# High and low activations side by side: one 512-column product for two of the three passes

## What is computed

```python
def swiglu_ffn(h, w_in, w_out):              # hidden width 5632, twice
    g, u = jnp.split(h @ w_in, 2, axis=-1)
    return (jax.nn.silu(g) * u) @ w_out
...
q = rms_norm((h @ w_q).reshape(b, s, N_X_HEADS, X_HEAD_DIM), q_g)
```

## Time and profile before

| | us |
|---|---|
| median of 3 runs | 3943.48 (3941.76 to 3947.19) |
| the profiled execution | 3947.24 |
| its span, first to last instruction | 3945.5 |
| PE busy (share of the span) | 3680.2 (93%) |
| DVE busy | 2140.2 (54%) |
| ACT busy | 1617.5 (41%) |

### The profile page before, as it was taken

One profiled execution on the slowest core, in us unless ns is written; L12 is line 12 of the kernel. 1 busy time (PEld: TensorE's weight loads), 2 busy tenths in 40 slices (PEclk: granted clock), 3 DMA queues, 4 the chain that ended last, 5 costly groups with the idle time before them and its releaser, 6 DMA issues.

```text
span 3945.5 us, 60283 instructions
## 1 busy us (share of the span) xinstructions
PE 3680.2 (93%) x24695; PEld 3366.3 (85%) x24695; DVE 2140.2 (54%) x2737; ACT 1617.5 (41%) x2144; POOL 241.6 (6%) x232
## 2 busy tenths in 40 slices
PE   7888799999997999989999999999989899999998
PEld 6766799999977997768989989899777699899897
DVE  5887634555656545555444444554555554444444
ACT  4334323655643333444433333343333354333333
POOL 3562000000000020000000000000000000000000
PEclk9988899999998999989999999999998899999999
DMA  7324456555454564435656656555324356566564
GB/s 207 97 86 145 136 150 181 140 151 149 139 192 124 175 160 128 150 107 149 175 183 184 182 186 180 184 164 160 124 90 135 101 159 181 181 181 181 182 185 144
DMA packets 859333, 612.34 MB, mean 155 GB/s; under 512 B 10370, under 2 KB 752305, under 8 KB 858144
## 3 DMA queue, kind: packets, MB, share of 16 engines
q1 hardware_dynamic: 857072, 602.21, 52.3%
q0 software_dynamic: 2096, 7.81, 0.7%
HBM read 607.82 MB, written 2.16 MB: 155 GB/s over the span
## 4 chain that ended last, share of the span: by engine, by line
PE 83%; DVE 9%; ACT 3%; issue 2%; POOL 2%; DMA 0%; ACTq 0%; DVEq 0%; SPq 0%
PE acc L897 48%; PE acc L887 27%; PE psC L990 2%; DVE wL L1658 2%; PE psA L959 1%; ACT wH L1256 1%; DVE xtok L1619 1%; PE psC L945 1%; DVE arena L1965 1%; PE psB L945 1%; PE psB L973 1%; ACT L1256 1%; POOL arena L760 0%; PE psA L862 0%; DMA xtok<-in_x 0%
## 5 line engine op out<-in xcount | busy, mean ns | idle before, releaser
L1658 DVE TENSOR_TENSOR wL<-ring,wH 128x1024 fp32r<-128x1024 f32 x1128 | 1336.4, 1226 | 1125.3 <-ACT wH L1256 1120.6
L897 PE MATMUL acc<-actH,wH 128*128 128x256 f32 x5760 | 1654.8, 287 | 28.4 <-DVE wL L1658 28.4
L897 PE MATMUL acc<-actL,wH 128*128 128x256 f32 x5760 | 1632.4, 283 | 0.0
L897 PE MATMUL acc<-actH,wL 128*128 128x256 f32 x5760 | 1632.1, 283 | 0.0
L1256 ACT CAST wH<-ring 128x1024 fp32r<-128x1024 f32 x1128 | 1125.1, 1046 | 1223.2 <-PE acc L887 631.9
L897 PEld LDWEIGHTS acc<-actH,wH 128*128 128x128 f32 x5760 | 1108.3, 192 | 40.7 <-DVE wL L1658 23.0
L897 PEld LDWEIGHTS acc<-actL,wH 128*128 128x128 f32 x5760 | 1108.3, 192 | 4.8 <-issue 3.3
L897 PEld LDWEIGHTS acc<-actH,wL 128*128 128x128 f32 x5760 | 1107.7, 192 | 0.0
L887 PE MATMUL acc<-wH,actH 128*128 128x512 f32 x896 | 365.5, 408 | 25.9 <-DVE actL L1650 22.8
L887 PE MATMUL acc<-wL,actH 128*128 128x512 f32 x896 | 356.6, 398 | 0.0
L887 PE MATMUL acc<-wH,actL 128*128 128x512 f32 x896 | 355.7, 397 | 0.0
(11 more groups left out here) (294 smaller groups left out, 2488.1 us busy)
## 6 DMA issues: line engine op xcount, KB each, us to landing
ring<-in_w_ffn_in SPq DMA_DIRECT2D x176, 1024.0 KB, 5.7
ring<-in_w_ffn_out SPq DMA_DIRECT2D x88, 1024.0 KB, 5.1
ring<-in_b_w_in SPq DMA_DIRECT2D x64, 1024.0 KB, 6.2
ring<-in_w_in_ab SPq DMA_DIRECT2D x56, 1024.0 KB, 5.5
ring<-in_w_in_c SPq DMA_DIRECT2D x48, 1024.0 KB, 5.7
ring<-in_kv_w SPq DMA_DIRECT2D x24, 1024.0 KB, 5.6
ring<-in_a_w_in SPq DMA_DIRECT2D x16, 1024.0 KB, 7.1
ring<-in_w_xkv SPq DMA_DIRECT2D x16, 1024.0 KB, 5.7
```

Of the source, the lines that this page charges most:

```text
L897: ins = pe.matmul(dst, w[:, t, f * P:(f + 1) * P], x[:, t, :], start=t == 0 and n == 0, stop=t == ph.kt - 1 and n == 2)
L1658: dve.tensor_tensor(wL[:, split_slot, cols], ring[:, slot, cols], wH[:, split_slot, cols].bitcast(F32), ALU.subtract).then_inc(l_made, 1)
```

## The change

280 of the 360 "feat" blocks (all whose chunk is not drained through a silu or through ACT, and all of `ffn_in`) become "joined". High and low activations now lie side by side in one tile `act2`. For each of the 16 row tiles there are two matmuls in place of three: the high weight times 512 columns (high and low activations), whose halves land in the left and right half of a bank, and the low weight times the 256 high columns, added into the right half. Each block has a bank of its own. The chunk leaves PSUM in two steps: ACT copies the left halves of both banks to SBUF (`take_left`), DVE then adds the right halves (`add_right`). In the FFN the gate goes through ACT, DVE and then ACT again (silu, now from SBUF); the value chunk through ACT (copy), DVE (add), DVE (times silu, from SBUF).

```diff
+        self.joined, self.joined0 = joined, plan["joined"]
...
+        act2 = sb("act2", P, FT, 2, T, dt=F32R)
+        actH, actL = act2[:, :, 0, :], act2[:, :, 1, :]
...
+        def take_left(act, ph, i, c, dst):
+            act.wait_ge(blocks_done, ph.blocks_before(i, c, ph.blocks))
+            first = 2 * ph.pair(c)
+            act.copy(dst, acc[:, first:first + 2, 0:T]).then_inc(left_out, 1)
+        def add_right(dve, ph, i, c, dst, left):
+            dve.wait_ge(left_out, ph.lefts(i, c))
+            first = 2 * ph.pair(c)
+            return dve.tensor_tensor(dst, left, acc[:, first:first + 2, T:2 * T], ALU.add)
...
+                elif ph.joined:                                            # PE
+                    bank = pair[:, b, :]
+                    for t in range(ph.kt):
+                        pe.matmul(bank.rearrange("p (h t) -> p h t", h=2), high[:, t, :], act2[:, t, :, :],
+                                  start=t == 0, stop=False)
+                        ins = pe.matmul(bank[:, T:2 * T], low[:, t, :], xH[:, t, :], start=False,
+                                        stop=t == ph.kt - 1)
...
+                if b == ph.blocks - 1 and ph.joined:                       # ACT, after its casts
+                    take_left(act, ph, i, c, feat_slot(ph, fn, i, c))
...
                     def finish(i, c):                                      # ACT, FFN
                         if c == 0:
                             wait_past(act, drained[ffn_in.pair(1)], ffn_in.pair_uses(i, 1))
-                            act.activation(silu_g, src, ACT.Silu).then_inc(drained[ffn_in.pair(0)], 1)
+                            take_left(act, ffn_in, i, 0, silu_g)
                         else:
+                            act.wait_ge(drained[ffn_in.pair(0)], ffn_in.pair_uses(i, 0) + 1)
+                            act.activation(silu_g, silu_g, ACT.Silu).then_inc(silu_done, 1)
+                            take_left(act, ffn_in, i, 1, up_left)
                             act.wait_ge(drained[ffn_in.pair(1)], ffn_in.pair_uses(i, 1) + 1)
                             act.activation(hidH[:, bass.ts(i, 2), :], hid_f, ACT.Identity).then_inc(hid_h, 1)
...
-                        dve.wait_ge(drained[ffn_in.pair(0)], ffn_in.pair_uses(i, 0) + 1)
-                        dve.wait_ge(blocks_done, ffn_in.blocks_before(i, 1, 2))
-                        dve.tensor_tensor(hid_f, silu_g,
-                                          acc[:, 2 * ffn_in.pair(1), :].rearrange("p (f t) -> p f t", t=T),
-                                          ALU.mult).then_inc(drained[ffn_in.pair(1)], 1)
+                            if c == 0:
+                                add_right(dve, ffn_in, i, 0, silu_g, silu_g).then_inc(drained[ffn_in.pair(0)], 1)
+                        add_right(dve, ffn_in, i, 1, hid_f, up_left).then_inc(up_summed, 1)
+                        dve.wait_ge(silu_done, i + (pairs_done + 1))
+                        dve.wait_ge(up_summed, i + (pairs_done + 1))
+                        dve.tensor_tensor(hid_f, hid_f, silu_g, ALU.mult).then_inc(drained[ffn_in.pair(1)], 1)
```

More of the change, by code:

```diff
@@ L124, with __init__ @@
 class Dense:
-    def __init__(self, plan, src, kt, cols, blocks, chunks, style, iters=1, hidden=False):
+    def __init__(self, plan, src, kt, cols, blocks, chunks, style, iters=1, hidden=False, joined=False):
         self.src, self.kt, self.cols, self.blocks, self.style = src, kt, cols, blocks, style
@@ L132, in __init__ @@
         plan["chunks"] += chunks
+        self.joined, self.joined0 = joined, plan["joined"]
+        plan["joined"] += chunks if joined else 0
         self.end = plan["chunks"]
@@ L287, in program @@
         xoT = area(1024, XH, T)
-        silu_g, hid_f = ffn_tmp[:, 0, :, :], ffn_tmp[:, 1, :, :]
+        silu_g, hid_f, up_left = (ffn_tmp[:, k, :, :] for k in range(3))
         A_RE, A_IM, A_DT, A_D, A_BGLU = 0, 32, 64, 96, 104
@@ L347, in program @@
         out_done = sem("out_done")
-        plan = {"blocks": 0, "chunks": 0}
+        plan = {"blocks": 0, "chunks": 0, "joined": 0}
         def columns(w, kt, cols):
@@ L354, in columns, with feat @@
             return lambda j, k=0: v[:, k * kt:(k + 1) * kt, bass.ts(j, cols)]
-        def feat(w, first, tiles, iters=1):
+        def feat(w, first, tiles, iters=1, joined=True):
             at = columns(w, FT, P)
@@ L369, in tok @@
                          "tok", iters, hidden)
-        s5_u = feat(a["a_w_in"][0], 0, 8, 2)
-        s5_z = feat(a["a_w_in"][0], 8, 8, 2)
-        kv_mem = [(feat(a["w_xkv_2"][l], 0, XH), tok(a["w_xkv_2"][l], 1, 1, 4)) for l in range(DEPTH)]
+        s5_u = feat(a["a_w_in"][0], 0, 8, 2, joined=False)
+        s5_z = feat(a["a_w_in"][0], 8, 8, 2, joined=False)
+        kv_mem = [(feat(a["w_xkv_2"][l], 0, XH, joined=False), tok(a["w_xkv_2"][l], 1, 1, 4)) for l in range(DEPTH)]
         glu_at = columns(a["a_w_glu"][0], 8, 2 * P)
@@ L383, in program @@
             b_q.append(feat(a["b_w_in"][0], 8 * hh, 8, 2))
-            b_z.append([feat(a["b_w_in"][0], NH * (r + 1) + 8 * hh, 8, 2) for r in range(BRANCHES)])
+            b_z.append([feat(a["b_w_in"][0], NH * (r + 1) + 8 * hh, 8, 2, joined=False) for r in range(BRANCHES)])
         nsa_counts = [1] * 16 + [2] * 8 + [1] * 24
@@ L1266, in one_block @@
                                   i * (16 * ph.body * ph.blocks // SLOTS) + 16 * (n // SLOTS + 1), n)
-                if b == ph.blocks - 1 and fn is not None:
+                if b == ph.blocks - 1 and ph.joined:
+                    take_left(act, ph, i, c, feat_slot(ph, fn, i, c))
+                elif b == ph.blocks - 1 and fn is not None:
                     drain_chunk(act, ph, i, c, fn)
@@ L1447, in _ @@
             turn_out(TURN_LN1)
-            alternate(head_roots(norm_mem), join(*(block_steps(ph) for ph in kv_cmp)), [2, 2, 2, 2])
+            alternate(head_roots(norm_mem), join(*(block_steps(ph, dst) for ph, dst in zip(kv_cmp, (kcT, vcT)))),
+                      [2, 2, 2, 2])
             act.copy(mark[:, :], consts[:, 0:1]).then_inc(h_made, 2 * len(W1_BLOCKS))
@@ L1462, in _ @@
                            ACT.Sigmoid).then_inc(gate_ready, 1)
-            for ph in kv[1:]:
-                dense(ph)
-            dense(b_q[0])
+            dense(kv[1])
+            dense(kv[2], kwT)
+            dense(kv[3])
+            dense(b_q[0], qT)
             def silu_z(k):
@@ L1480, in _ @@
             alternate(attend(nsa_units), join(*(
-                [block_steps(b_z[0][r], silu_z(r)) for r in range(BRANCHES)] + [block_steps(b_q[1])] +
+                [block_steps(b_z[0][r], silu_z(r)) for r in range(BRANCHES)] + [block_steps(b_q[1], qT)] +
                 [block_steps(b_z[1][r], silu_z(BRANCHES + r)) for r in range(BRANCHES)])), nsa_counts)
@@ L1545, in tail_act @@
                                               i * 16 + 16 * (n // SLOTS + 1), n)
[L1546 to L1547 removed]
+                            finish(i, c)
                     pairs_done += ffn_in.iters
@@ L1553, in _ @@
             turn_out(TURN_MIX[1], G_MIX + 16)
-            dense(c_q)
-            blocks = join(block_steps(c_k), block_steps(c_v))
+            dense(c_q, dqT)
+            blocks = join(block_steps(c_k, dkT), block_steps(c_v))
             alternate(head_roots(norm_c), blocks, [2] * 8 + [1] * 4)
@@ L1665, in one_block @@
                     split_weights(n % SLOTS, n % SPLIT_SLOTS, ph.blocks_before(i, c, b) + 1)
-                if b == ph.blocks - 1 and fn is not None:
+                if b == ph.blocks - 1 and ph.joined:
+                    dst = feat_slot(ph, fn, i, c)
+                    add_right(dve, ph, i, c, dst, dst).then_inc(drained[ph.pair(c)], 1)
+                elif b == ph.blocks - 1 and fn is not None:
                     drain_chunk(dve, ph, i, c, fn)
```

33 lines of the change are left out of this document (20 added, 13 removed).

## The result

| | before | changed |
|---|---|---|
| median of 4 runs, us | 3942.62 | 4022.42 |
| lowest to highest | 3940.23 to 3947.19 | 4008.05 to 4026.12 |
| ratio, 95% interval | | 1.0194 (1.0167 to 1.0221) |
| span of the profiled execution | 3945.5 | 4022.5 |
| its mean granted clock | 0.967 | 0.954 |

A forecast was written before the change was run, and what follows sets the result against it. PE's matmul stream was taken as the bound. FFN +23.0, outside the FFN -6.9, clock +4.2 and +6.5 sum to +26.8 us, giving 3970 us on the median; range 3942 to 3996.

The forecast's parts named there:

- The matmuls: Joined blocks: 0.3474 us a pair, so 5.558 us a block in place of 5.760; 280 blocks save 56.6 us.
- The chain at the end of an iteration: FFN-in iteration ends, drain 1.47 us longer: +26.4 us over 24 boundaries (parts 2, 3), +23.4 over 14 (part 1).
- E: In an FFN-in iteration, the end of the value chunk's last matmul, from which the prediction counted PE's restart.
- The change to FFN-out: Ahead of each FFN-out PE waits for the low part, which comes 1.47 us later, 6 times: +8.8 us.
- Outside the FFN: Among head norms PE waits 0.64 us longer, 22 times: +14.1 us, against -21.0 from matmuls there: net -6.9.
- The clock: Longer PE stops lower the granted clock: +4.2 us at FFN-outs, +6.5 (bounds 0 and 20) at part 1's 14 stops.
- 16.1: Whole kernel with the clock left where it is, a rival: +16.1 us, 3959.6; chance 0.24.
- That rival: Every longer stop of PE lowers the clock: +39.9 us, 3983 us; chance 0.14.

The follow-up runs named there:

- x9: Changed kernel, its banks and drains kept, with the wide product split again into two of 256 columns; ratio 1.0294 to the kernel before.
- x4: Kernel before with only the 104 blocks outside FFN-in joined, FFN-in as before; ratio 1.0059 to the kernel before.
- x10: Changed kernel plus 8 unread 128-column matmuls in each head-norm step where PE waits for the drained chunk; ratio 1.0220 to the kernel before.
- x1: Changed kernel plus unread 512-column matmuls where PE waits in the FFN's first part and ahead of every FFN-out; ratio 1.0126 to the kernel before.
- x2: Changed kernel with the eight blocks of `kv_cmp` left unjoined, as before; ratio 1.0146 to the kernel before.
- x7: Kernel before plus one silu of one column on ACT ahead of the FFN's first loop; ratio 1.0005 to the kernel before.
- x12: Kernel before with FFN-in and 48 other blocks joined, early silu, second block's weight split earlier, products grouped in twos, unread matmuls ahead of FFN-out: ratio 0.9886, 3900.6 us.
- x5: Changed kernel with the products of two row tiles grouped as wide, wide, narrow, narrow; ratio 1.0152 to the kernel before.

## Why the prediction was wrong

The sign and the price of the drains were right, the size was not: 26.8 us forecast, 77 to 80 measured, outside the range. Two terms failed, the price of a pair and above all the clock. By the prediction's own steps:

- **The matmuls.** -56.6 forecast, from 0.3474 us a pair. That price exists (0.3467), but 177 of 280 blocks ran at 0.3533, at 0.107 a block saved in place of 0.202. Measured about -38. An error of 19 us, and one that I could not read before: no row had the mixture, and my bounds (5.12 to 5.76 us a block) held the value, 5.65. From the Trainium skill, TensorE: Matmul & The Clock Gate, section Back-to-back issue gap, I had estimated a saving of 0.04 us a block, which puts a block near 5.72 (5.76 less 0.04). Both measured blocks, 5.55 and 5.65, lie under it. The section gives its gap for an isolated matmul, which the prediction did not say.
- **The chain at the end of an iteration.** Right, but for the wait of 0.92 in place of 1.10 in parts 2 and 3. Part 2: PE restarts at E + 6.36 (forecast 6.40). Part 1: ACT's copy stands at 1873.58 in the chain, so E is 1873.49, and PE restarts at 1881.27, E + 7.78 (forecast 7.83):

```profile
1873.58 0.60 ACT ffn_tmp L546
...
1876.51 1.25 ACT L1289
...
1881.27 0.50 PE acc L918
```

- **The change to FFN-out.** Right: E is 2307.69 by the copy in the chain, PE starts at E + 4.22, where I had said some 4.2.

```profile
2307.78 0.59 ACT ffn_tmp L546
...
2310.88 0.70 DVE hidL L2179
2311.91 1.10 PE acc L911 x2
```

- **Outside the FFN.** The 0.64 per drain is there; at `kv_cmp`'s end, for instance, copy, sum and diagonals follow one another. x9 bears out the drains as a whole. The net of -6.9 became +23 (x4): fewer microseconds from the pairs, and the clock.

```profile
503.09 0.59 ACT arena L546
503.71 0.69 DVE arena L552
504.52 0.69 DVE probT L1739
```

- **The clock: the step that failed.** I took 4.2 + 6.5 = 10.7, with 19.6 as the upper bound of the part that I let vary. Measured +42 by the distances, +48.6 by halves. At FFN-out I had the count right (all six), but they cost 7.7 us more (492.8 together against 485.2), not 4.2, for some lost up to 2.8. I had the fourteen ends of part 1 as one in three at 1.4 us; seven of fourteen fell, at some 1.7 us (16 pairs of 0.460 in place of 0.353), 12 us. That is 20 in the FFN. What I left out, at nothing and without a reason, was everything else. I had priced waits among head norms by their length alone, 0.64 each, and not asked what they do to the clock: at `cmp_w1` and in the first `b_q` they cost some 14 us (the stretch is +16.5, and x10 with the same drains has +2.8; `cmp_w1` alone 10.5), and some 9 around `c_k` and `c_v` (+14.0, where x4 with the same instructions has +4.6). I also took 1.4 us as the price of any fall, from FFN-outs where PE streams at once; at `cmp_w1` the clock stayed at 0.50 for the whole of 27 us, though PE ran matmul after matmul. Why it does is open.

The sum with the measured sizes is 16.1 + 19 + 42 = 77 (84 with the clock by halves), against 77 in the profiles. That they meet to the microsecond is luck: at the 38 ends of iterations the slower block runs while PE would wait for `wL` anyway, which takes some 4 us off, and the clock's term is good to a few. That longer or added waits lower the clock is shown by x1, x2, x9 and x10; why the same instructions keep it in one run and lose it in another (x4, x7) is open.

Of what the Trainium skill describes in TensorE: Matmul & The Clock Gate, section HAM oscillation — how this bites in real kernels, a clock that falls at every wait between bursts, I had said that the trace agrees in part. It still does so in part: the clock fell at six of six changes to FFN-out, at seven of fourteen ends in part 1, where that rule has fourteen and I had between four and five, and in none of the second and third parts, although PE waits some 0.9 us in each of their iterations. That rival's 3983 us was nearer than my 3970, but neither held the waits outside the FFN.

## What to carry to other kernels

A wait of PE has two prices, its length and what the clock loses after it; the second was the larger here, some 42 us of 77. Read the granted clock at every place where a change lengthens a wait, not only at the longest ones, and look at what stands behind: after the waits before FFN-out the clock cost 1.4 to 2.8 us, ahead of `cmp_w1` 10.5. Where a drain gets longer, first move what PE needs next ahead of it (x12: 22.30 us an iteration in place of 23.53), and fill a wait that stays with unread matmuls, but only there.

## What the runs showed of the hardware

- Products of 512 and 256 columns one by one in turn run at 0.3467 or at 0.3533 us a pair, and keep to one of them until PE stands still or other matmuls come between; in groups of two they run at 0.3483, in all 268 blocks of x5 and all 224 of x12.
- At the lower clock (1.2 GHz) such a pair takes 0.64 us, less than twice its time at 2.4 GHz.
- Unread matmuls in a wait hold the clock: FFN-out 87.33 us in place of 89.56 after a wait of 4.2 us, and the like at all six (x1).
- A gain in one place can go with a lower clock elsewhere: in x7, 12 us won and some 12 to 16 us of clock lost, most of it in stretches with the same instructions.
- Entering a loop with the table that its body ends with took two table loads of 1.28 us out of each iteration (111 loads before, 81 in x7).
